# GpSimd and VectorE add the squares of the RMS norms, and TensorE multiplies one summed tile with ones

## The reference

```python
def rms_norm_2(x, g):
    y = xf * lax.rsqrt(jnp.mean(xf * xf, axis=-1, keepdims=True) + RMS_EPS)
    return (y * g.astype(jnp.float32)).astype(x.dtype)
...
def swiglu_ffn(x, w_in, w_out):
    gate, up = jnp.split(x @ w_in, 2, axis=-1)
    return (jax.nn.silu(gate) * up) @ w_out
```

## Time and profile before

| | us |
|---|---|
| median of 3 runs | 2102.28 (2101.6 to 2103.04) |
| profiled execution | 2104.61 |
| its span | 2102.8 |
| TensorE busy | 2066.4 |
| VectorE busy | 1042.2 |
| ScalarE busy | 812.2 |
| GpSimd busy | 14.3 |

### The profile page before, as it was taken

How to read it: one execution, slowest core, us unless ns; L and a number is a source line. 1 busy time by engine, 2 the same in 40 slices (tenths; PEclk the granted TensorE clock), 3 DMA queues, 4 the chain that set the end, 5 groups by cost and what they waited for, 6 DMA issues and landing times.

```text
span 2102.8 us, 26809 instructions
## 1 busy us (share of the span) xinstructions
PE 2066.4 (98%) x10736; PEld 1728.0 (82%) x10736; DVE 1042.2 (50%) x1812; ACT 812.2 (39%) x1353; POOL 14.3 (1%) x28
## 2 busy tenths in 40 slices
PE   8999999999999999999999999999899999999998
PEld 6788888888877787789988888898788798888887
DVE  6656444434354254344644442367687655444323
ACT  5634333323314333333433322344677653333222
POOL 0000000000000000000000000000000000000000
PEclk9999999999999999999999999999899999999999
DMA  4223233333322232222233333343011022333332
GB/s 158 80 61 107 83 100 91 100 93 93 112 86 71 67 99 65 79 92 91 82 100 100 92 93 101 96 155 114 28 42 41 12 91 81 100 94 97 93 101 68
DMA packets 53547, 184.50 MB, mean 88 GB/s; under 512 B 6010, under 2 KB 8330, under 8 KB 53168
## 3 DMA queue, kind: packets, MB, share of 16 engines
q1 hardware_dynamic: 50976, 171.99, 26.8%
q0 software_dynamic: 2160, 10.63, 1.5%
q10 hardware_dynamic: 288, 0.17, 0.0%
HBM read 180.62 MB, written 2.14 MB: 87 GB/s over the span
## 4 chain that ended last, share of the span: by engine, by line
PE 90%; DVE 4%; ACT 2%; issue 1%; DVEq 0%; ACTq 0%
PE bank L489 68%; PE bank L509 6%; PE bank L649 6%; PE bank L1019 2%; PE bank L883 2%; PE bank L1001 1%; DVE WL L1629 1%; PE bank L873 1%; PE bank L986 1%; PE bank L987 1%; ACT WH L1079 0%; PE bank L686 0%; DVE XT L2059 0%; PE bank L776 0%; PE bank L592 0%
## 5 line engine op out<-in xcount | busy, mean ns | idle before, releaser
L1629 DVE TENSOR_TENSOR WL<-RAW,WH 128x1024 fp32r<-128x1024 f32 (+1 forms) x320 | 384.0, 1204 | 509.9 <-ACT WH L1079 509.2
L489 PE MATMUL bank<-AH,WH 128*128 128x512 f32 x1456 | 573.4, 397 | 2.8 <-DVE T L2248 2.4
L489 PE MATMUL bank<-AL,WH 128*128 128x512 f32 x1456 | 566.7, 393 | 0.0
L489 PE MATMUL bank<-AH,WL 128*128 128x512 f32 x1456 | 565.4, 392 | 0.0
L1079 ACT ACTIVATE WH<-RAW 128x1024 fp32r<-128x1024 f32 (+1 forms) x320 | 331.4, 1041 | 540.2 <-PE bank L489 443.7
L489 PEld LDWEIGHTS bank<-AH,WH 128*128 128x128 f32 x1456 | 275.4, 190 | 60.7 <-DVE T L2248 3.3
L489 PEld LDWEIGHTS bank<-AH,WL 128*128 128x128 f32 x1456 | 275.9, 190 | 58.8
L489 PEld LDWEIGHTS bank<-AL,WH 128*128 128x128 f32 x1456 | 275.8, 190 | 55.8 <-issue 0.7
L1683 DVE TENSOR_TENSOR T<-bank,RS 128x512 f32<-128x512 f32 x156 | 106.2, 686 | 178.6 <-PE bank L489 178.6
L489 PE MATMUL bank<-HH,WH 128*128 128x512 f32 x484 | 188.3, 389 | 0.0
L489 PE MATMUL bank<-HLO,WH 128*128 128x512 f32 x484 | 188.3, 389 | 0.0
(11 more groups left out here) (370 smaller groups left out, 2788.4 us busy)
## 6 DMA issues: line engine op xcount, KB each, us to landing
RAW<-in_ffn_in SPq DMA_DIRECT2D x132, 512.0 KB, 3.6
RAW<-in_ffn_out SPq DMA_DIRECT2D x48, 512.0 KB, 3.5
RAW<-in_ret_t SPq DMA_DIRECT2D x32, 512.0 KB, 3.6
RAW<-in_ffn_out SPq DMA_DIRECT2D x24, 384.0 KB, 3.1
RAW<-in_ret_v SPq DMA_DIRECT2D x16, 512.0 KB, 3.8
RAW<-in_ret_out SPq DMA_DIRECT2D x16, 512.0 KB, 3.6
RAW<-in_w_in_t SPq DMA_DIRECT2D x13, 512.0 KB, 3.7
RAW<-in_nsa_t SPq DMA_DIRECT2D x9, 512.0 KB, 3.6
```

The costliest lines, as they stand in the source:

```text
L489: t = e.matmul(BANK[b][:, :], wt[:, sl], xx[:, slot(kk) if name == "nsa_out" else kk, :], start=kk == 0 and n == 0, stop=kk == kt - 1 and ...
L1629: e.tensor_tensor(WL[w][:, 0:n], RAW[r][:, 0:n], WH[w][:, 0:n], ALU.subtract).then_inc(w_low.did(v))
```

## The change

The sums are completed before TensorE sees them. VectorE adds the last square too in f1, in the heads, in `row_sums_of_both` and in `half_row_sums`; only the last half sum of the kernel, ("end3", 1), keeps the last square apart, and its wait for that square stands behind the first product. In an opening GpSimd adds the squares (`add_squares`), 14 additions of 128x256, and TensorE multiplies once (`stream_sums`), after the fifth matmul of the fifth tile; the pair adds and the reduction go. The half sums are asked for one half part later. On ScalarE the silu and the weight unit of a head go ahead of the copies of OR. At the end the gain ffn_post1 is applied in ScalarE's copy of ffn3_out, VectorE's `scale` is then a plain product, and GpSimd does three of the eight last additions to the stream.

```diff
+ON_GPSIMD = (1, 3, 5)
...
-                    e.wait_ge(*stream.at(("out", f, h)))
+                    e.wait_ge(*(summed.at(("out", f)) if h and f in ON_GPSIMD else stream.at(("out", f, h))))
...
+            add_squares(e, "f2", "ret")
             e.wait_ge(*matmul.at(("ffn2_out", 7)))
...
             e.memset(VC[:, :, :, :], 0.0).then_inc(zeroed.did("vc"))
+            add_squares(e, "kv", 2)
             e.wait_ge(s_scr, 16)
...
-            e.wait_ge(*matmul.at(("sums", "kv", 3, 1)))
+            e.wait_ge(*matmul.at(("sums", "kv")))
             bias_table(e, 0)
...
+            add_squares(e, "f3", "nsa")
+            for f in ON_GPSIMD:
+                e.wait_ge(*scaled.at(("end3", f, 1)))
+                e.tensor_tensor(XT[:, f, H[1]], XT[:, f, H[1]], M[3][:, f, H[1]], ALU.add).then_inc(
+                    summed.did(("out", f)))
+        def add_squares(e, st, key):
+            for h in range(2):
+                total = M[key][:, 0, H[h]]
+                for f in range(1, 8):
+                    e.wait_ge(*squared.at((st, f, h)))
+                    if f > 1:
+                        e.wait_ge(*summed.at((st, f - 1, h)))
+                    e.tensor_tensor(total, total, M[key][:, f, H[h]], ALU.add).then_inc(summed.did((st, f, h)))
...
-                    if n == done + 1:
+                    if n == done + 2:
                         half_row_sums(st, 0)
-                    if n == done + 4:
+                    if n == done + 5:
                         half_spread(st, 0)
...
-                        if m == 0 and h == 0 and kk == 2:
+                        if m == 1 and h == 0 and kk == 2:
                             half_row_sums(branch, 1)
                         if m == 1 and h == 0 and kk == 4:
                             half_spread(branch, 1)
-                        k = 8 * h + kk
-                        if m == 1 and k > 4 and k % 2:
-                            half_pair_sums(st, (k - 5) // 2 % 4, (k - 5) // 8, key)
...
-                    if n in (1, 3):
-                        half_pair_sums(st, 2 + n // 3, 1, key)
+                    if n == 4:
+                        stream_sums(st, key)
...
-                e.wait_ge(*added.at((st, 6, h)))
-                e.wait_ge(*squared.at((st, 7, h)))
+                apart = (st, h) == ("end3", 1)
+                e.wait_ge(*added.at((st, 6 if apart else 7, h)))
                 for tt in (2 * h, 2 * h + 1):
-                    e.matmul(BANK[4][:, tt:tt + 1], ACC[:, ROWS[tt]], ones[:, :], start=True, stop=False)
-                    t = e.matmul(BANK[4][:, tt:tt + 1], SQ[1][:, ROWS[tt]], ones[:, :], start=False, stop=True)
+                    t = e.matmul(BANK[4][:, tt:tt + 1], ACC[:, ROWS[tt]], ones[:, :], start=True, stop=not apart)
+                    if apart:
+                        e.wait_ge(*squared.at((st, 7, h)))
+                        t = e.matmul(BANK[4][:, tt:tt + 1], SQ[1][:, ROWS[tt]], ones[:, :], start=False, stop=True)
                 t.then_inc(matmul.did(("sums", st, h)))
...
+            def stream_sums(st, key):
+                enter(7, ("sums", st))
+                e.wait_ge(*summed.at((st, 7, 1)))
+                for tt in range(4):
+                    t = e.matmul(BANK[7][:, tt:tt + 1], M[key][:, 0, ROWS[tt]], ones[:, :], start=True, stop=True)
+                t.then_inc(matmul.did(("sums", st)))
...
-                e.wait_ge(*added.at((st, n - 2)))
+                e.wait_ge(*added.at((st, n - 1)))
                 for tt in range(4):
-                    if tt == 0:
-                        e.matmul(BANK[4][:, 0:1], ACC[:, ROWS[0]], ones[:, :], start=True, stop=False)
-                        e.wait_ge(*squared.at((st, n - 1)))
-                    else:
-                        e.matmul(BANK[4][:, tt:tt + 1], ACC[:, ROWS[tt]], ones[:, :], start=True, stop=False)
-                    t = e.matmul(BANK[4][:, tt:tt + 1], SQ[1][:, ROWS[tt]], ones[:, :], start=False, stop=True)
+                    t = e.matmul(BANK[4][:, tt:tt + 1], ACC[:, ROWS[tt]], ones[:, :], start=True, stop=True)
                 t.then_inc(matmul.did(("sums", st)))
...
-                e.wait_ge(*squared.at(("gained", 7)))
-                e.wait_ge(*added.at(("gained", 6)))
-                for at, total, last in ((0, ACC, SQ[1]), (4, SUM2, SQ2[1])):
+                e.wait_ge(*added.at(("end1", 7)))
+                e.wait_ge(*added.at(("gained", 7)))
+                for at, total in ((0, ACC), (4, SUM2)):
                     for tt in range(4):
-                        column = BANK[4][:, at + tt:at + tt + 1]
-                        e.matmul(column, total[:, ROWS[tt]], ones[:, :], start=True, stop=False)
-                        t = e.matmul(column, last[:, ROWS[tt]], ones[:, :], start=False, stop=True)
+                        t = e.matmul(BANK[4][:, at + tt:at + tt + 1], total[:, ROWS[tt]], ones[:, :], start=True,
+                                     stop=True)
...
-                    e.wait_ge(*free_v.at(("sums", st)))
-                    e.activation(rtok[:, 0:4], sums[:, 0:4], ACT.Sqrt, bias=eps, scale=1.0 / 1024).then_inc(
-                        rooted.did(st))
+                    e.wait_ge(*matmul.at(("sums", st)))
+                    e.activation(rtok[:, 0:4], BANK[7][:, 0:4], ACT.Sqrt, bias=eps, scale=1.0 / 1024).then_inc(
+                        free_a.did(("sums", st)))
...

...
-                e.activation(M[key][:, f, :], BANK[b][:, :], ACT.Copy).then_inc(free_a.did((name, f)))
+                if gain:
+                    e.activation(M[key][:, f, :], BANK[b][:, :], ACT.Copy, scale=V(gain, f)).then_inc(
+                        free_a.did((name, f)))
...
                 before("ret_t", 8 * h + 4)
+                ret_silu(e, h, 0)
+                before("ret_t", 8 * h + 5)
                 for et in range(4):
                     e.wait_ge(*matmul.at(("or", h, et)))
                     if h > 0 and et == 0:
                         e.wait_ge(*gate_v.at(("ret", 4 * h - 1)))
                     e.activation(OR[:, et, :], BANK[4 + et][:, :], ACT.Copy).then_inc(free_a.did(("or", h, et)))
-                ret_silu(e, h, 0)
-                before("ret_t", 8 * h + 5)
                 for et in range(4):
...
-            def reduce_sums(st, bank, last):
-                e.wait_ge(*matmul.at(last))
-                e.tensor_reduce(sums[:, :], BANK[bank][:, 0:16].rearrange("p (a f) -> p a f", f=4), AX_X,
-                                ALU.add).then_inc(free_v.did(("sums", st)))
...
                 add_to_stream("w_out", f)
                 low("f1", f, "norm2")
-                if 0 < f < 7:
+                if f:
                     add_square("f1", f)
...
+            def half_adds(name, st, h, last=False):
                 tiles = HALVED[K_TILES[name]]
-                for f in tiles[:-1]:
+                for f in (7,) if last else tiles[:-1]:
                     half_add_square(st, f, h, f == tiles[0])
...
                 half_adds(name, st, 0)
+                half_adds(name, st, 0, last=True)
                 half_invert(st, 0)
...
                 for k in range(1, 16):
                     if k < 15:
                         update(*at(k + 1))
-                    if k > 4 and k % 2:
-                        half_add_pair(st, (k - 5) // 2 % 4, (k - 5) // 8, key)
                     if k < 14:
                         scale(*at(k + 2))
                     half_low(st, *at(k), gain)
@@ -2032,14 +2040,12 @@
                         ahead(p.first[to, 1])
                     if k == 2:
                         half_adds(name, branch, 1)
+                        ahead(p.first[to, 2])
                     if k == 3:
-                        ahead(p.first[to, 2])
+                        half_adds(name, branch, 1, last=True)
                     if k == 4:
                         ahead(p.first[to, 3])
                         half_invert(branch, 1)
-                half_add_pair(st, 2, 1, key)
-                half_add_pair(st, 3, 1, key)
-                reduce_sums(st, 7, ("sums", st, 3, 1))
...
-                if 0 < f < 7:
+                if f:
                     add_square("end1", f)
                     add_gained(f)
...
-                for f in (1, 2):
+                for f in range(1, 4):
                     add_square(("head", h), f)
...
+                e.tensor_tensor(M[3][:, f, H[h]], M[3][:, f, H[h]], BANK[5 - h][:, H[h]], ALU.mult).then_inc(
+                    scaled.did(("end3", f, h)))
...
+            for f in range(8):
+                scale(f, 0)
+                if f:
+                    update(f - 1, 0)
+                if f == 6:
+                    half_invert("end3", 1)
+            update(7, 0)
+            scale(0, 1)
+            for f in range(1, 8):
+                scale(f, 1)
+                if f - 1 not in ON_GPSIMD:
+                    update(f - 1, 1)
+            update(7, 1)
```

(25 more changed lines are left out.)

41 lines of the change are left out of this document (16 added, 25 removed).

## The result

| | before | after |
|---|---|---|
| median, us | 2102.05 (4 runs, 2101.6 to 2103.04) | 2091.14 (4 runs, 2089.34 to 2091.87) |
| ratio | | 0.9945, 95% interval 0.9933 to 0.9957 |
| profiled execution, us | 2104.61 | 2090.46 |
| its span | 2102.8 | 2088.7 |

The account below looks back on a forecast made before the run. TensorE, busy 98% of the span, was taken as the bound. Gains of 29.7 us less 3.3 and 0.4 lost gave 26.0, hence a 2076.3 us median; forecast 2071 to 2082, range with rivals 2069 to 2094.

Parts of the forecast that it names:

- Block sums, half sums, openings (17.4): Fewer products with `ones` on TensorE's queue: 6.2 us from block sums, 3.1 from half sums, 8.1 from three openings.
- Waits of the heads (2.9): TensorE's waits before the four heads' sums go because ScalarE's silu and weight copy move ahead; 2.9 us gained.
- the cover of 0.6 us for the add of square 3: In head 0, add 3 ends at 640.7 and TensorE comes at 641.3, so the added wait is covered.
- Clock (6.8): Granted-clock falls after `row_sums_of_both` and in heads 0 and 2 vanish with shorter sums; 6.8 us gained, bounds 0 and 6.8.
- WL in the openings (1.5): In the openings, the third tile's WL subtraction comes one step earlier, removing TensorE's three waits for WL; 1.5 us gained.
- GpSimd beside VectorE (3.3): In the openings, GpSimd's adds hold back VectorE and make TensorE wait; 1.1 us per opening, 3.3 us lost in all.
- Rivals 1 and 3: GpSimd and VectorE exclude each other in openings: 2089 us, chance 0.20; or clock falls too, slower than before, 0.08.
- Second half sums ("nothing is added"): In the openings, the second half's sum and spread move one half part later behind ready work; no added time.
- First half sums (0.4): At four branch ends the first half sum waits for the add of square 7; 0.1 us each, 0.4 us lost.
- tail (1.1): At the kernel's end, one product leaves the chain and VectorE does fewer operations; 1.1 us gained, bounds -0.4 and 1.6.
- Rivals 2 and 4: Clock still falls at shortened sums, 2083 us; or heads' reordering fails, keeping waits and clock falls, 2084.3; together chance 0.09.
- rival 1: In the openings GpSimd and VectorE exclude each other, with adds near the upper bound; 2089 us, chance 0.20.

Follow-up runs that it names:

- slot_kept: The kernel after with an unused 128x4 tile where the kernel before had `sums`, so tiles behind keep their places; 2077.28 us.
- before_moved32: The kernel before with an unused 128x8 tile ahead of `origin`, moving the tiles behind `sums` by 32 bytes; 2118.15 us.
- heads_old: Against slot_kept, ScalarE's old order in the retention: copies of OR ahead of the silu and weight unit; 2085.57 us.
- slot_plus64: The kernel after with an unused tile of 96 bytes per partition in the place of `sums`; 2081.45 us.

## Why the prediction was wrong in size

The first numbers are the prediction's, the last two the difference between the starts in the kernel before and in the other over the same stretch of TensorE's timeline.

| stretch | forecast | slot_kept | after |
|---|---|---|---|
| f1 | 0.9 | 0.9 | 0.9 |
| `row_sums_of_both` with its clock | 3.5 | 3.4 | 3.4 |
| head 0, wait and clock | 6.1 | 6.0 | 6.0 |
| heads 1 to 3 | 5.5 | 5.7 | 5.8 |
| three openings with their half sums | 8.7 | 9.6 | 9.6 |
| last branch end and tail | 1.4 | 2.1 | 2.1 |
| first matmuls, and falls of the clock in the attention | - | -1.6 | -1.0 |
| stages with displaced operands | - | 0 | -12.6 |
| sum, rounded | 26.0 | 26.1 | 14.1 |

- **The step that failed** is "nothing" where the sum has no line: what the deleted lines held besides their instructions. I priced the reduction of `reduce_sums` as an operation and never looked at its tile, and no part of the prediction asked what is allocated behind it. The runs showed 12.6 us lost in its place: 2067 matmuls longer by 0.0066 us, 13.6 in all, and matmuls of 128x256 shorter by about 1. The kernel before had the price in its rows, 396 ns beside 390 in w_out and 0.2312 us beside 0.2267 in ffn1_in (above); the prediction did not ask why.
- **Block sums, half sums, openings (17.4)**: right, 0.2225 us per product and 0.09 per block.
- **Waits of the heads (2.9)**: right, and shown by undoing the one edit; the cover of 0.6 us for the add of square 3 held.
- **Clock (6.8)**: right in sum between the profiled executions, and in part luck. Behind `row_sums_of_both` the fall goes with the number of products. In heads 0 and 2 the same wait and the same products show it in one execution and not in another (before_moved32), so that 5.1 of the 6.8 us can be there or not; heads_old brought the one of head 0 back, and not that of head 2. What decides in the heads stays open.
- **WL in the openings (1.5)**: gone; no half matmul waits for WL, and none for AH or AL by more than 0.1 us.
- **GpSimd beside VectorE (3.3)**: too dear. An addition takes 0.83 us and not the 0.62 that I took; it lay inside the bounds. The estimate by the Trainium skill's factor of 1.96 (GPSIMD Engine Reference, Performance versus the Vector engine), 0.82, was right. But adding up GpSimd's busy time, 11.6 us, overstated the 2.7 us that VectorE loses by four, and TensorE lost 0 to 0.3 us per opening instead of 1.1. Rivals 1 and 3 fall with it; the point from which the exclusion costs lies between 14 and 28 additions.
- **Second half sums ("nothing is added")**: wrong. They gained nothing where 0.4 us each was forecast. Each starts 0.29 to 0.64 us after the matmul ahead of it, where it was 0.12, and two of them wait 0.36 us for VectorE's last addition; that is 1.5 us in all. So the three openings gave 0.9 us more than forecast, and not some 2.4.
- **First half sums (0.4) and tail (1.1)**: 2.1 together against 1.4; VectorE's last adds were not held back (0.41 us), so 0.3 was taken off for nothing.

Rivals 2 and 4 did not occur in the profiled execution. The time after, 2091.14, is near the 2089 of rival 1 by chance: no wait of that kind stands in its trace. The kernel that the prediction described is slot_kept, 2077.28 us against 2076.3.

## What to carry to other kernels

When a diff adds or drops a tile, list the tiles allocated behind it and what TensorE reads from them: here 32 bytes took half of a gain of 26 us. Where matmuls of 128x512 bound the kernel, keep moving operand and weights at a distance that is a multiple of 256 bytes (0 and -256 were tried), with a named unused tile or an explicit alignment, and compare the matmuls' distance from start to start in stages that nobody edited before any other reading of a result. The lock between GpSimd and VectorE is to be costed by VectorE's operations that it lengthens, not by GpSimd's busy time. The version that beats both kernels is the change with the slot kept: 2077.28 us, and 2074.4 to 2076.2 in the three other layouts with the same distances.

## What the runs showed of the hardware

- The distance from start to start of a 128x512 matmul depends on the start of the moving tile relative to that of the weights, with a period of 256 bytes: 0.2267 us at 0, 0.2289 at +64, 0.2321 to 0.2333 at 128, 0.2333 at +32, -32 and -64. Whole stages keep one value. It is not the whole rule: at +64, w_out of slot_plus64 took 0.2333 where its ffn1_out took 0.2289. The mechanism isn't shown; no stage was run at +96 or -96, nor at a distance within 32 bytes. Matmuls of 128x256 follow each other at 0.120 us at 0 and at 0.113 to 0.120 elsewhere, so they become no longer.
- GpSimd's addition of 128x256 takes 0.83 us in the mean, 0.89 in most of those beside VectorE's lows. In each opening three of VectorE's 16 additions then take 0.88 to 0.96 us instead of 0.42, eight lows 0.57 instead of 0.48, and one low 0.96.
- The granted clock fell behind 16 one-column products in two of three executions of the same kind, and behind a wait of 1.6 us with eight of them in one of two: one profile without a fall doesn't show that a stretch is safe, and one with a fall doesn't show that an edit removed it.
